# A hybrid decoder step in one program: the front part's attention moved ahead of the block compression and run as one sequence

## The reference, cut to what matters

```
z = x @ W_in                                   # 512 prompt tokens (4 tiles of 128) and 32 sample tokens
mix = [NSA(z_nsa) ; mLSTM(z_mlstm)]
h = LayerNorm(ALPHA * x + mix @ W_out)
y = LayerNorm(ALPHA * h + PEER(h))
...
def nsa(q, k, v):                              # 8 query heads, head dim 64, 2 KV heads
    kc = compress(k_cmp, pe, w1, b1, w2)       # blocks of 32 tokens, stride 16: gelu(flat @ w1 + b1) @ w2
    vc = compress(v_cmp, pe, w1, b1, w2)
    o_cmp = softmax(q @ kc^T * scale) @ vc     # 31 blocks for the prompt
    o_sel = causal softmax attention over the selected blocks
    o_win = causal softmax attention over a window of 512
    return g0 * o_cmp + g1 * o_sel + g2 * o_win
def mlstm_chunk(C, n, m, q, k, v, i, f):       # also updates the sample states C, n: C' = w*C + k v^T
def PEER(h):                                   # 8 heads, product keys: top 16 of 128 + 128, top 16 of 256,
    gather 128 expert rows u, v of 1024 floats for each token; sum gelu(h . u_e) * g_e * v_e
```

## Time and profile before

| | us |
|---|---|
| three runs: median (lowest to highest) | 2391.7 (2376.59 to 2399.35) |
| the profiled execution: time | 2383.09 |
| its span in the trace | 2381.2 |
| mean granted TensorE clock, share of full speed | 0.837 |
| PE, DVE, ACT, POOL busy, share of the span | 75%, 67%, 19%, 53% |
| first gather issued on POOL | 715.15 |

### The profile page before, as it was taken

How to read it: one execution, slowest core, us unless ns; L and a number is a source line. 1 busy time by engine, 2 the same in 40 slices (tenths; PEclk the granted TensorE clock), 3 DMA queues, 4 the chain that set the end, 5 groups by cost and what they waited for, 6 DMA issues and landing times.

```text
span 2381.2 us, 20283 instructions
## 1 busy us (share of the span) xinstructions
PE 1797.0 (75%) x6550; PEld 1062.8 (45%) x6550; DVE 1589.9 (67%) x3264; ACT 463.7 (19%) x1078; POOL 1259.7 (53%) x1129
## 2 busy tenths in 40 slices
PE   7999772988855888758696889869968676376554
PEld 4433451966752434323364657547743334122210
DVE  2330571042297889968768998898778787667876
ACT  1110110022113425211111121111115142010110
POOL 0000000000007777876777787887777777666775
PEclk9999775556987989879798989979989898698677
DMA  3111506030219999999999999999999999999997
GB/s 130 71 71 57 38 5 235 19 142 0 89 71 357 381 382 380 339 390 395 398 395 407 410 351 380 396 376 385 411 408 399 411 409 407 414 385 407 366 372 288
DMA packets 201433, 698.14 MB, mean 293 GB/s; under 512 B 37680, under 2 KB 49648, under 8 KB 192816
## 3 DMA queue, kind: packets, MB, share of 16 engines
q0 software_dynamic: 161504, 604.58, 65.4%
q1 hardware_dynamic: 39824, 92.27, 11.4%
HBM read 690.38 MB, written 10.55 MB: 294 GB/s over the span
## 4 chain that ended last, share of the span: by engine, by line
POOL 35%; PE 16%; DVE 13%; issue 11%; DMA 11%; SPq 1%; ACT 1%; POOLq 0%; DVEq 0%; ACTq 0%
POOL arena L774 18%; POOL arena L786 17%; PE bank L807 13%; DMA arena<-in_uv,arena 8%; DVE arena L2025 3%; PE bank L2116 2%; DVE arena L2043 1%; DVE arena L1775 1%; PE bank L819 1%; POOL arena L753 1%; DVE arena L1772 1%; DMA arena<-in_w2pad 1%; DMA arena<-in_w_pq 1%; DMA arena<-in_kwin 1%; DVE arena L1777 1%
## 5 line engine op out<-in xcount | busy, mean ns | idle before, releaser
L807 PE MATMUL bank<-arena 128*128 128x512 f32 (+14 forms) x4740 | 1366.6, 449 | 476.9 <-DMA arena<-in_uv,arena 292.7
L807 PEld LDWEIGHTS bank<-arena 128*128 128x128 f32 (+4 forms) x4740 | 804.9, 203 | 995.7 <-issue 698.6
L774 POOL DMA_INDIRECT arena<-in_uv,arena x544 | 611.3, 1124 | 530.4 <-DVE arena L1833 333.8
L2025 DVE CUSTOM_DVE_ANT_0 arena<-arena 128x1024 f32<-128x1024 f32 x544 | 649.5, 1226 | 230.9 <-DMA arena<-in_uv,arena 224.0
L786 POOL DMA_INDIRECT arena<-in_uv,arena x544 | 612.7, 1126 | 185.6 <-issue 157.9
L2043 DVE SCALAR_TENSOR_TENSOR arena<-arena 128x1024 f32<-128x1024 f32 x274 | 352.1, 1285 | 37.8 <-DMA arena<-in_uv,arena 28.5
L2116 PE MATMUL bank<-arena 128*128 128x512 f32 (+13 forms) x972 | 314.6, 484 | 44.5 <-DMA arena<-in_w_in 14.3
L1631 ACT ACTIVATE arena<-arena 128x128 f32<-128x128 f32 (+1 forms) x265 | 90.9, 389 | 850.2 <-DVE arena L2035 850.1
L2116 PEld LDWEIGHTS bank<-arena 128*128 128x128 f32 (+3 forms) x972 | 159.7, 199 | 198.8 <-issue 161.1
L739 POOL DMA_DIRECT2D arena<-out_p_kc x2 | 1.4, 686 | 376.7 <-DMA out_p_vc<-arena 376.7
L819 PE MATMUL bank<-arena 128*128 128x128 f32 (+3 forms) x732 | 120.8, 305 | 45.8 <-ACT arena L1334 17.4
(11 more groups left out here) (234 smaller groups left out, 771.6 us busy)
## 6 DMA issues: line engine op xcount, KB each, us to landing
arena<-in_w_pq SPq DMA_DIRECT2D x10, 2048.0 KB, 10.4
arena<-in_uv,arena POOLq DMA_INDIRECT x1088, 8.3
arena<-in_w_in SPq DMA_DIRECT2D x6, 2048.0 KB, 7.8
arena<-in_w_out SPq DMA_DIRECT2D x6, 2048.0 KB, 12.0
arena<-in_w SPq DMA_DIRECT2D x4, 2048.0 KB, 12.9
arena<-in_w_pq SPq DMA_DIRECT2D x8, 1024.0 KB, 18.5
arena<-in_subk SPq DMA_DIRECT2D x3, 1024.0 KB, 8.9
arena<-in_xT SPq DMA_DIRECT2D x1, 2176.0 KB, 8.5
```

What stands on the lines that cost most here:

```text
L774: nc.gpsimd.indirect_dma_start(uv[buf(h, r)][:, 0:D], None, half_rows, bass.IndirectOffsetOnAxis(eidx_u[:, t, s0 + r:s0 + r + 1], 0))\
L807: return te.matmul(out, l, r, start=start, stop=stop)
L2025: last = ve.tensor_tensor_reduce(out=uv[b][:, 0:D], in0=uv[b][:, 0:D], in1=x_sb[:, t, :], scale=1.0, scalar=0.0, op0=ALU.mult, op1=ALU.add ...
```

## The change

1. **`s_C` leaves the gate.** Its write has a semaphore of its own (`s_sc`) and is issued after the W1 loads instead of before the key and value rows. Only POOL's first chunk loads and the end of the program wait for it. The front of the other engines waits for `s_p2w` without it.
2. **Order on TensorE.** The 9 fills of q and k come before the 11 pieces of the state update (now in banks 0 and 1). ScalarE no longer waits for `s_omix` ahead of them; VectorE's memset of `QP` moves to the start of the program.
3. **Attention before compression.** The 32 units of tiles 0 and 1 run as one sequence ahead of the wait for W1. Scores go through four banks (4, 5, 0, 1), probabilities and their transposes through four quarters of their buffers. In step st TensorE does the scores of unit st, the transposes of unit st-3 and the product of unit st-4.
4. **Compressed attention of both tiles together.** Scores of both tiles in banks 0 and 1, then each engine does its step for tile 0 and tile 1; `combine` is from banks 4 and 5.
5. **Projection.** The transposes of `mix[1]` come after the projection of tile 0; tile 0 projects into banks 0 and 1, tile 1 into 2 and 3, so tile 1 no longer waits for tile 0's variance.
6. **Queries and scores by quarters.** One loop of 9 steps over both tiles: a quarter of the query projection, then the key scores of the quarter before. The transposes of tile 1's h come after the second quarter. `hT` has a buffer for each tile. VectorE's steps c of `retrieve(0)` wait for quarter 1 + c // 2 alone. POOL's wait for `s_sf` moves behind the first `load_u`.

```diff
-        P2W = 16 * (1 + KC + 4)
+        P2W = 16 * (1 + KC + 3)
+        s_sc = sem("sample_C_written")
...
+        PX_u = [PX.rearrange("p z s -> p (z s)")[:, 256 * k:256 * k + 256] for k in range(4)]
+        PT_u = [PTb.rearrange("p z s -> p (z s)")[:, 256 * k:256 * k + 256] for k in range(4)]
...
                 sp.dma_start(w2k[:, n], i["w2pad"][n].rearrange("(m p) d -> p m d", p=P)).then_inc(s_w1, 16)
+            sp.wait_ge(s_cue, 11)
+            sp.dma_start(o["s_C"].rearrange("p (g v) -> p g v", g=32), C0).then_inc(s_sc, 16)
...
             pe_eng.wait_ge(s_rope, TILES)
-            pe_eng.wait_ge(s_p2w, P2W)
-            pe_eng.wait_ge(s_omix, 1)
+            pe_eng.wait_ge(s_ce, MH)
...
+            pe_eng.wait_ge(s_vb, 1)
+            pe_eng.wait_ge(s_kse, 1)
+            pe_eng.wait_ge(s_bce, 1)
+            for n in range(11):
+                if n >= 2:
+                    pe_eng.wait_ge(s_cue, n - 1)
+                c0, c1 = n * 387, min(32 * 129, (n + 1) * 387)
+                mm(PB[n % 2][:, 0:c1 - c0], kws, VBf[:, c0:c1]).then_inc(s_cup, 1)
+
+            pe_eng.wait_ge(s_omix, 1)
+            S_BANK = (4, 5, 0, 1)
+            N_U = 2 * UNITS
+            for st in range(N_U + 4):
+                if st < N_U:
+                    br, t, h = PU[st]
+                    if st >= 4:
+                        pe_eng.wait_ge(s_px, st - 3)
+                    elif st >= 2:
+                        pe_eng.wait_ge(s_cue, 11)
+                    r = slice(HD * (h // NG), HD * (h // NG) + HD)
+                    mm(PB[S_BANK[st % 4]][:, 0:(t + 1) * P], QT[r, h % NG, t * P:(t + 1) * P],
+                       KT[r, br, 0:(t + 1) * P]).then_inc(s_s, 1)
+                if 3 <= st < N_U + 3:
+                    u = st - 3
+                    pe_eng.wait_ge(s_px, u + 1)
...
+                    unit_filled[u] = fill(p_fill)
+                if 4 <= st:
+                    u = st - 4
+                    pe_eng.wait_ge(s_te, unit_filled[u])
...
+                        last = mm(PB[2 + bt % 2][:, h * HD:(h + 1) * HD], PT_u[u % 4][:, k * P:(k + 1) * P],
+                                  zkv[k][:, c:c + HD], k == 0, k == t)
+                    last.then_inc(s_pv, 1)
 
             pe_eng.wait_ge(s_w1, 80)
+            pe_eng.wait_ge(s_px, N_U)
...
+            for t in range(2):
+                pe_eng.wait_ge(s_cou, t + 1)
+                fl = fill8(mix[t], P)
+                if t == 0:
+                    pe_eng.wait_ge(s_wo, 32)
                 pe_eng.wait_ge(s_te, fl)
+                for _ in project(P, mixT_b[:, t], wout_b, PB[2 * t:2 * t + 2]):
+                    pass
+
+            order = [(0, q4) for q4 in range(4)] + [(1, q4) for q4 in (3, 2, 1, 0)]
+            pe_eng.wait_ge(s_h, 1)
+            fl = fill8(x_sb[:, 0, :], P)
+            for nq in range(9):
+                if nq < 8:
...
+                if nq == 1:
+                    pe_eng.wait_ge(s_h, 2)
+                    fl = fill8(x_sb[:, 1, :], P)
+                    pe_eng.wait_ge(s_sk, 16)
+                if nq >= 1:
+                    q4 = order[nq - 1][1]
+                    pe_eng.wait_ge(s_qe, nq)
+                    if nq >= 5:
+                        pe_eng.wait_ge(s_se, nq - 4)
...
+            act.wait_ge(s_omix, 1)
+            for st in range(N_U + 1):
+                if st < N_U:
+                    act.wait_ge(s_nb, st + 1)
...
+                    sc.activation(PX_u[st % 4][:, 0:L], PB[(4, 5, 0, 1)[st % 4]][:, 0:L], ACT.Exp,
+                                  bias=nbu[:, st % 4:st % 4 + 1], scale=SCALE,
+                                  accum_out=rsu[:, (st // NH) % 2, h:h + 1]).then_inc(s_px, 1)
+                if st >= 1:
...
+                    drain(PT_u[u % 4][:, 0:L], lambda b: b[:, 0:L])
...
+            std("in", 0, P)
+            drain8(hT[0], P)
+            std("in", 1, P)
...
+            for st in range(N_U + 6):
+                if st < N_U:
+                    dve.wait_ge(s_s, st + 1)
+                    bank = PB[(4, 5, 0, 1)[st % 4]]
+                    link(ve.tensor_tensor(bank[:, t * P:L], bank[:, t * P:L], C("caus"), ALU.add))
+                    link(ve.reduce_max(mx1[:, 3:4], bank[:, 0:L], axis=AX))
...
-                    dve.wait_ge(s_se, (4, 8, 9 + c // 2, 12, 13)[t])
+                    dve.wait_ge(s_se, (1 + c // 2, 8, 9 + c // 2, 12, 13)[t])
...
             for t in range(2):
                 dve.wait_ge(s_mo, t + 1)
-                layer_norm("in", t, PB).then_inc(s_h, 1)
+                layer_norm("in", t, PB[2 * t:2 * t + 2]).then_inc(s_h, 1)
```

More of the change, by code:

```diff
@@ L365, in program @@
         pq = Place(half_at)
-        hT = pq.take(1024).rearrange("p (c s) -> p c s", c=KC)
+        pq.take(1024)
+        hT = [arena[:, front + k:front + k + 1024].rearrange("p (c s) -> p c s", c=KC) for k in (0, 3072)]
         subk_b = pq.take(2048).rearrange("p (g k) -> p g k", g=16)
@@ L949, in cmp_attend @@
                 last.then_inc(s_cs, 1)
-                yield
+            for t in range(2):
                 pe_eng.wait_ge(s_cpn, t + 1)
@@ L1453, in rest_scalar @@
                 drain8(mixT_b[:, t], P)
-            for t in range(2):
-                std("in", t, P)
-            for t in range(2):
-                query(t)
+            std("in", 0, P)
+            drain8(hT[0], P)
+            std("in", 1, P)
+            order = [(0, q4) for q4 in range(4)] + [(1, q4) for q4 in (3, 2, 1, 0)]
+            for nq in range(9):
+                if nq < 8:
+                    t, q4 = order[nq]
+                    act.wait_ge(s_qf, nq + 1)
+                    if t:
+                        act.wait_ge(s_sf, q4 + 1)
+                    sc.activation(qpT[:, 4 * q4:4 * q4 + 4, :],
+                                  PB[nq % 2][:, :].rearrange("p (g s) -> p g s", g=4), ACT.Copy).then_inc(s_qe, 1)
+                if nq == 1:
+                    drain8(hT[1], P)
+                if nq >= 1:
+                    t, q4 = order[nq - 1]
+                    act.wait_ge(s_sf, nq)
+                    sc.activation(SC[t][:, 4 * q4:4 * q4 + 4, :],
+                                  PB[2 + (nq - 1) % 4][:, :].rearrange("p (g k) -> p g k", g=4), ACT.Copy)\
+                      .then_inc(s_se, 1)
             gate_exp(0)
@@ L1716, in cmp_attend @@
-            def cmp_attend(t):
-                sh = [P, NH, PBLK]
-                dve.wait_ge(s_cs, t + 1)
+            sums = [c8, gs8]
+            shc = [P, NH, PBLK]
+            for t in range(2):
+                dve.wait_ge(s_cs, 2)
                 for n in range(NKV):
-                    last = ve.tensor_tensor(PX_c[:, NG * n:NG * n + NG, :],
-                                            PB[4 + n][:, 0:NG * PBLK].rearrange("p (h c) -> p h c", h=NG),
+                    scores = PB[n][:, NG * t * PBLK:NG * (t + 1) * PBLK].rearrange("p (h c) -> p h c", h=NG)
+                    last = ve.tensor_tensor(PX_cu[t][:, NG * n:NG * n + NG, :], scores,
@@ L2105, in _ @@
             sp.dma_start(o["p_C"], Cout).then_inc(s_p2w, 16)
-            sp.wait_ge(s_cue, 11)
-            sp.dma_start(o["s_C"].rearrange("p (g v) -> p g v", g=32), C0).then_inc(s_p2w, 16)
             rest_sync(sp)
@@ L2324, in _ @@
             settle(s_pad)
+            ve.memset(QP.rearrange("p b r -> p (b r)"), 0.0).then_inc(s_qp, 1)
+            settle(s_qp)
             dve.wait_ge(s_const, 32)
```

250 lines of the change are left out of this document (75 added, 175 removed).

## The result

The changed kernel takes 2304.66 us, median of 4 runs (2302.15 to 2306.73), against 2389.36 us, median of 4 runs of the kernel before (2376.59 to 2399.35): a ratio of 0.9658, 95% interval 0.9635 to 0.968 (the two medians alone give 0.9646), 84.7 us less. The profiled execution took 2305.76 us with a span of 2303.9 us. The kernel is faster, and the forecast was 2315 us.

What follows compares the result with a forecast made beforehand. A front of about 715 us before POOL's first gather was the part to shorten; the back follows unchanged. Savings of 47 (waits, fills), 10 (attention), 4 (projection), 17 (queries) and 0.7 made 78.6 us: forecast 2315 us, range 2289 to 2342.

Steps and rivals of the forecast that it cites:

- three signs of being wrong: First gather to end moves over 15 us; attention's second half at 1.3 us a unit; TensorE load wait between 433 and 552.
- Waits and fills, 47 us: Front before attention: 47 us saved from the waits for s_C and W1 and the fills placed beside VectorE.
- Attention, 63 us: 32 units of tiles 0 and 1: 16 x 1.25 + 16 x 2.5 + 3 = 63 us, ending at 433.
- Bias and compression: After attention: same instructions, 27.4 us of bias and 37 us of compression, ending at 497.5 us.
- Compressed attention 22 us: After compression, both tiles interleaved: 22 us until TensorE is at mix[0], at 519.5 us.
- Projection 32.7 us: After compressed attention: 32.7 us instead of 36.7, ending at 552.2 us.
- Queries to POOL 84.2: From projection's end to POOL's first gather: 84.2 us, 16.7 less, with the gather at 636.5 us.
- The round trip that holds the units apart: Rival, attention: each unit takes its whole way, 162 us instead of 63, kernel 2414 us; chance 2%.
- The cold projection: Rival, projection and queries: clock stays at 1.2 GHz, +68 us, kernel 2383 us; chance 3%.
- The back: Rival, from first gather to end: gives back 20 to 45 us, kernel 2335 to 2360 us; chance 12%.
- The clock rises in the attention: Rival, attention: full clock halves tile 1's units to 1.26 us, kernel 2291 us; chance 15%.

Runs made afterwards that it cites:

- u2: Changed kernel with the s_C write issued in its old place, ahead of the weight loads, which wait for it again; 2303.75 us, ratio 0.9653.
- b1: Kernel before, with only the s_C write moved behind the W1 loads, on its own semaphore; 2351.45 us, ratio 0.9836.
- u1: Changed kernel, but TensorE waits for the W1 weights before the attention; 2314.55 us, ratio 0.9695.
- u3: Changed kernel, but attention with two score banks, two buffers and the old lags; 2310.71 us, ratio 0.9667.
- u4: Changed kernel, but VectorE waits for all four groups of scores before its first top-16 maximum; one run, 2326.09 us.
- v4: Changed kernel with the bias folded into the hidden products and an unused 256-column product in each tile 0 attention unit only; 2243.39 us, ratio 0.942.
- w1: Changed kernel with hidden products widened from 62 to 124 columns by unused zeros, bias products kept; one run, 2279.45 us.
- c2: Changed kernel with an unused 256-column product ahead of each attention unit's score product, in both tiles; 2299.08 us, ratio 0.9627.
- v3: Changed kernel with the bias folded into the hidden products and an unused 256-column product in each tile 1 attention unit only; 2275.82 us, ratio 0.9545.
- v1: Changed kernel with the 128 one-column bias instructions folded into hidden products of 124 columns; 2264.84 us, ratio 0.9492.
- v2: Changed kernel with the bias folded into the hidden products and an unused 256-column product in every attention unit of both tiles; 2252.64 us, ratio 0.9446.

## Why the prediction was right

| step | predicted, us | measured |
|---|---|---|
| attention starts | 370 | 369 to 370.5 |
| weights landed | 386.9 | 381.5 |
| attention ends, bias starts | 433 | 428.5 |
| bias and compression end | 497.5 | 492.5 |
| TensorE at mix[0] | 519.5 | 511.54 |
| projection ends | 552.2 | 545.15 |
| first gather | 636.5 | 631.83 |
| from there to the end | 1,666 | 1672.1 |

None of the three signs of being wrong showed: the last stretch moved by 6.0 us and not 15, tile 1 ran at 2.51 us a unit and not 1.3, and TensorE waited for no load. The closeness is in part luck. The forecast was 8 us late at mix[0], because attention and compressed attention were priced too high; the queries then took 2.5 us more than forecast, and the 4.7 us by which the first gather came early met a back that was 6.0 us longer.

**Waits and fills, 47 us: right in size.** The attention starts where VectorE's chain ends, 369 us, and no wait is left. The weights landed 5 us earlier than worked out, with 47 us of slack, and u2 spends 40 us of it unharmed. But the forecast did not say what each part was worth, and the runs show two that overlap: b1 gets 36.3 by the order alone, and u1 loses only 12.9 without the cover. 36.3 and 12.9 make 49.2. The fills' new place beside VectorE is inside those 12.9 and was not undone by itself, nor were the changes to the compressed attention and the projection.

**Attention, 63 us: 59.5 us (369 to 428.5), with the wrong floor in tile 0.** Tile 1 at 2.51 us a unit is inside the bounds of 2.2 to 2.52, at the end at which nothing is gained: TensorE was full there already, as the earlier trace rows said. Tile 0 was taken at 1.25 us, from a floor of 1.13 and a round trip that deeper buffers would hide. At the clock of 0.50 it takes 1.455 with TensorE busy 10.00 of 10 us, so there was hardly a round trip to hide: the 1.13 had priced the four instructions beside the transpose by those of one column, 0.214 us, and 1.455 - 0.27 leaves 0.30 for each. The earlier trace rows showed it, TensorE at 9.96 of 10 us in the old tile 0. That miss alone would have made the attention longer, 16 x 1.455 + 16 x 2.51 = 63.4 us and 3 for start and end. It came out at 59.5 because the first four units took 0.88 us each while the clock was still up from the state pieces (2.3 us), which the sum did not have, and because the start and end cost nothing extra: three scores are issued ahead of the first transposes, and the last units, with no score left to do, took 1.17 us. These misses cancelled, which is luck. The depth bought some 5 us by one profile (u3).

**Bias and compression: 64 us against 64.5.** Same instructions, same clock, same time.

**Compressed attention 22 us: 19.** The 32 score instructions took 4.5 us and not 6.9, from the first one at 492.55 to the wait of 3.85 us ahead of 500.88: 0.14 us each. They had been priced by the bias instructions' 0.214 us. The wait for VectorE's and ScalarE's steps, 3.85 us, was the 3.7 of the forecast.

**Projection 32.7 us: 33.6**; the granted clock was still 0.64 in 510 to 520 us, at the start of the first product. **Queries to POOL 84.2: 86.7.** VectorE started at +18.8 (18.3 predicted), but the groups came 8.04, 8.04 and 8.6 us apart and not 7.5, so VectorE began the last one at +43.5 and not +41; the rest, 43.2 us, was as in the forecast. u4 prices the overlap at 17.1, and 16.7 was the sum's.

**The rivals.** The round trip that holds the units apart did not come: units ran at 1.455 us, and u3, with half the depth, still at 1.52. The cold projection did not come: 1.00 from 520 us on. The back gave nothing that stands out of its spread. *The clock rises in the attention* is the one that I weighed too simply. It did not rise; it was at 0.99 and fell. The argument against it, the same units at 0.50 with TensorE full, was sound for this kernel, and it was no proof that those units can't run at 1.00: v4 has them there. The Trainium skill, page "TensorE: Matmul & The Clock Gate", section "HAM oscillation — how this bites in real kernels", advises for thin matmuls to arrange the loop so that no wait for a load falls between them, or to pad them. The trace agrees with the padding in w1, c2 and v4 (13.92 us down to 9.49 and 7.41, a unit from 2.51 us to 1.88 and 1.39), and does not in v3, where the padded units stayed at 0.50 and cost 3.47 us each. A wait for a load is not what brought the low clock here: TensorE was busy 10.00 of 10 us from 380 to 450 us at 0.50.

## What to carry to other kernels

Before covering a wait for a load with work, look at what stands ahead of the load in its queue: here one output write, waiting for a late value, held the weights back, and moving it alone gave 36 us of 85. In a chain of small float32 matmuls count the instructions and read the granted clock beside the busy share: a full engine at 0.50 is not at its limit, and fewer, wider instructions, or even useless columns at the one place where the clock would fall, can be worth more than a deeper pipeline (39 and 21 us of first gather against 5, starts taken off). The same padding in the wrong place cost time (v3, from the start to the first gather 19 us more than v1). When parts are tested by undoing them one at a time, undo the pair as well: two parts that each look cheap to remove can be covers for each other.

## What the runs showed of the hardware

A granted clock of 1.00 or 0.50 persisted under identical, gapless work: tile 1's padded unit took 1.88 us in v2 and 3.47 us in v3, its unpadded one 2.51 us in the changed kernel and 1.39 us in v4. Each held for the whole tile, in one profile of each kernel. Other work moved the clock: the products of 124 columns brought it from 0.50 to 1.00 in w1, and in c2 it fell from 1.00 to 0.50 at about 427 us, among the one-column bias instructions. Sixty-four product instructions of 62 columns took 13.92 us at 0.50, sixty-four of 124 columns 7.41 us at 1.00. A float32 matmul instruction of one column and one of 62 cost the same at 0.50, 27.44 / 128 = 0.214 and 13.92 / 64 = 0.217 us, so between these sizes an instruction has a price and its columns have none. The weight loads (PEld) beside them were busy 10.00 of 10 us as well, 48 in 10 us, so the price may be that of loading 128x128 weights; no run separates the two. The compressed scores, 64 rows deep and 31 columns wide, took 0.14 us each, the compressed products, 31 rows deep, 0.22; why is not shown. And the start of the attention moved by 5.6 us between profiles of the changed kernel and its variants, which do the same work up to it, with the granted clock of 340 to 370 us between 0.60 and 0.72; that is why differences of the first gather under 5 us are read here with the start beside them.
